# A routed expert layer on one core: the down matrix laid out eight rows per partition and brought in one transfer, the activations transposed in 64 by 64 blocks

## The reference

```python
def expert_block(args):
    xb, e = args
    gu = xb @ w_gu[e] + b_gu[e]                 # 1024 x 2048 per expert, 8 MB
    g = jnp.minimum(gu[:, :D_EXPERT], SWIGLU_LIMIT)
    lin = jnp.clip(gu[:, D_EXPERT:], -SWIGLU_LIMIT, SWIGLU_LIMIT)
    glu = g * jax.nn.sigmoid(SWIGLU_ALPHA * g)
    return ((lin + 1.0) * glu) @ w_down[e] + b_down[e]   # 1024 x 1024 per expert, 4 MB
```

## Time and profile before

| | |
|---|---|
| median of 3 runs | 1186.44 us (1186.06 to 1187.45) |
| profiled execution | 1186.64 us |
| its span | 1184.9 us |
| granted TensorE clock, mean of the span | 0.982 |
| PE busy | 1101.6 us (93%) |
| PEld busy | 582.4 us (49%) |
| DVE busy | 392.4 us (33%) |
| ACT busy | 247.0 us (21%) |
| moved by DMA | 452.07 MB, mean 382 GB/s |

### The profile page before, as it was taken

The page is one execution under the profiler, slowest core; times in us unless marked ns, Lnnn a source line. Parts: engine busy times, 40 slices in busy tenths (PEclk is TensorE's granted clock), DMA queues, the critical chain, the costliest instruction groups (busy, mean ns, idle before and its releaser), DMA issues.

```text
span 1184.9 us, 14766 instructions
## 1 busy us (share of the span) xinstructions
PE 1101.6 (93%) x6066; PEld 582.4 (49%) x6066; DVE 392.4 (33%) x649; ACT 247.0 (21%) x389; POOL 4.5 (0%) x10
## 2 busy tenths in 40 slices
PE   8999999999999898989889898899899988998995
PEld 8999999984433333333333333333343333333331
DVE  6768655563222222222222222222222222222223
ACT  6444773432111111111111111111111111111112
POOL 0000000000000000000000000000000000000000
PEclk9999999999999999999999999999999999999998
DMA  9984444689999999999999999999999999999996
GB/s 328 349 280 159 160 161 159 252 320 402 416 414 431 430 430 431 430 431 431 431 436 428 428 436 429 428 435 429 428 435 429 427 436 423 430 431 430 414 424 257
DMA packets 60407, 452.07 MB, mean 382 GB/s; under 512 B 3490, under 2 KB 34455, under 8 KB 40535
## 3 DMA queue, kind: packets, MB, share of 16 engines
q1 hardware_dynamic: 59696, 449.79, 91.9%
q0 software_dynamic: 560, 1.74, 0.5%
q10 hardware_dynamic: 119, 0.08, 0.0%
HBM read 450.53 MB, written 1.06 MB: 381 GB/s over the span
## 4 chain that ended last, share of the span: by engine, by line
DMA 50%; PE 45%; SPq 1%; ACT 1%; DVE 1%; issue 1%; DVEq 0%
DMA dring<-in_w_down_dram 43%; PE bank L1146 17%; PE bank L1497 13%; PE bank L1444 10%; DMA ring<-in_w_gu_dram 6%; PE bank L1411 1%; DMA ring<-in_w_mem_kv_dram 1%; PE bank L1356 1%; PE bank L1237 0%; PE bank L1458 0%; PE bank L1386 0%; SPq L310 0%; ACT w_high L472 0%; PE bank L1549 0%; PE bank L1258 0%
## 5 line engine op out<-in xcount | busy, mean ns | idle before, releaser
L1444 PE MATMUL bank<-ring,region_x 128*64 128x512 f32 x2048 | 456.0, 597 | 6.6 <-DMA ring<-in_w_gu_dram 6.6
L1497 PE MATMUL bank<-dring,region_r 128*64 128x512 f32 x1024 | 245.1, 628 | 61.2 <-DMA dring<-in_w_down_dram 60.6
L1444 PEld LDWEIGHTS bank<-ring,region_x 128*64 128x64 f32 x2048 | 141.4, 137 | 280.7 <-issue 265.8
L1497 PEld LDWEIGHTS bank<-dring,region_r 128*64 128x64 f32 x1024 | 73.2, 143 | 230.2 <-issue 130.8
L1146 PE MATMUL bank<-hT_high,w_high 128*128 128x256 f32 x384 | 109.9, 286 | 1.3 <-DVE hT_low L727 1.3
L1146 PE MATMUL bank<-hT_high,w_low 128*128 128x256 f32 x384 | 108.7, 283 | 0.0
L1146 PE MATMUL bank<-hT_low,w_high 128*128 128x256 f32 x384 | 108.7, 283 | 0.0
L735 DVE TENSOR_TENSOR w_low<-ring,w_high 128x2048 fp32r<-128x2048 f32 x39 | 89.3, 2289 | 52.5 <-ACT w_high L472 52.4
L1052 DVE TENSOR_SCALAR region_r<-bank 128x512 f32<-128x512 f32 x32 | 22.1, 691 | 253.7 <-PE bank L1444 253.7
L1071 DVE SCALAR_TENSOR_TENSOR y_parts<-bank,region_r,y_parts 64x512 fp32r<-64x512 f32 x32 | 23.8, 744 | 224.0 <-ACT y_parts L644 224.0
L472 ACT ACTIVATE w_high<-ring 128x2048 fp32r<-128x2048 f32 x39 | 74.5, 1912 | 55.7 <-PE bank L1146 51.2
(11 more groups left out here) (241 smaller groups left out, 863.1 us busy)
## 6 DMA issues: line engine op xcount, KB each, us to landing
ring<-in_w_gu_dram SPq DMA_DIRECT2D x52, 4096.0 KB, 26.3
dring<-in_w_down_dram SPq DMA_DIRECT2D x56, 2048.0 KB, 25.1
ring<-in_w_gu_dram SPq DMA_DIRECT2D x17, 2048.0 KB, 11.5
ring<-in_w_in_dram SPq DMA_DIRECT2D x26, 1024.0 KB, 11.8
dring<-in_w_down_dram SPq DMA_DIRECT2D x16, 1024.0 KB, 11.9
ring<-in_w_gu_dram SPq DMA_DIRECT2D x14, 1024.0 KB, 7.9
ring<-in_w_out_dram SPq DMA_DIRECT2D x4, 1024.0 KB, 4.7
ring<-in_w_mem_kv_dram SPq DMA_DIRECT2D x3, 1024.0 KB, 12.3
```

What stands on the lines that cost most here:

```text
L1444: last = mm(ps[64 * half:64 * half + 64, :], xg[u // 2][:, c, 64 * (u % 2):64 * (u % 2) + 64], ring[:, slot0 + c, k * F + half * 512:k * F ...
L1497: last = mm(ps[64 * half:64 * half + 64, :], lhsT, dring[:, c // 2, at:at + 512], start=(c == 0), stop=(c == KC - 1))
```

## The change

A partition of `dring` held, for each half of the down matrix, four of its rows (4p to 4p+3 of that half). Now partition p holds rows 8p to 8p+7 of the whole matrix. The matrix is one run of 32 KB per partition, and `expert_down` brings it in one transfer of 4 MB instead of two of 2 MB, when all four pieces of the matrix before are used. The 1 MB pieces at the start and the end remain, with the new rows.

The left operand of `down` must follow: partitions 0 to 63 of a chunk need the activations of the first 512 columns, 64 to 127 those of the last 512. These are the halves in which `g_sb` has them. So `hidden_transposed` transposes 64 by 64 blocks, the lower half to the lower partitions, the upper to the upper: 16 ordinary products with a part of the identity in place of 4 transposes. L1059 writes with a stride of 8 instead of 4 at its source. In `small_products`, and at the last expert, the slots are now transposed ahead of the activations.

```diff
-            m, k = j // 2, j % 2
             sp.dma_start(dring[:, j:j + n, :].rearrange("p k n -> p (k n)"),
-                         a["w_down"][0, bass.ds(expert, 1), m * 512:(m + 1) * 512, :]
-                         .rearrange("e (p k) n -> p (e k n)", k=4)[:, k * PIECE:(k + n) * PIECE]).then_inc(down_in[j], 16)
-
-        def expert_down(expert, uses, n=2):
+                         a["w_down"][0, bass.ds(expert, 1), :, :]
+                         .rearrange("e (p k) n -> p (e k n)", k=KC)[:, j * PIECE:(j + n) * PIECE]).then_inc(down_in[j], 16)
+
+        def expert_down(expert, uses, n=DRING):
...
-            dve.tensor_tensor(hid_by_row, hid_fours, sg_fours, ALU.mult).then_inc(hid_ready, 1)
+            dve.tensor_tensor(hid_by_row, hid_eights, sg_eights, ALU.mult).then_inc(hid_ready, 1)
...
-            for c in range(4):
-                last = transpose(tr_ps[:, c * P:(c + 1) * P], g_sb[:, c * P:(c + 1) * P], ident)
+        def hidden_transposed():
+
+            for c in range(KC):
+                for m in range(2):
+                    half = slice(64 * m, 64 * m + 64)
+                    last = mm(tr_ps[half, 64 * c:64 * c + 64], g_sb[half, 64 * c:64 * c + 64], ident[half, half],
+                              start=True, stop=True)
             last.then_inc(hidT_done, 1)
...
             s = i * 4 + u
-            hidden_transposed(s, halves)
+            pe.wait_ge(hid_ready, s + 1)
+            pe.wait_ge(xg_sb, s + halves)
             pe.wait_ge(y_ready, s + 1)
             slots_transposed(s, y_ps)
+            hidden_transposed()
             scatter_of(s - 1, (u + 1) % 2)
...
             for c in range(KC):
-                if c % 4 == 0:
-                    pe.wait_ge(down_in[c // 2], (s + 1) * 16)
+                if c == 0:
+                    pe.wait_ge(down_in[0], (s + 1) * 16)
                 elif c % 2 == 0:
                     pe.wait_ge(down_in[c // 2], 16 + 16 * single)
-                lhsT = hidT[:, (c % 4) * P + 64 * (c // 4):(c % 4) * P + 64 * (c // 4) + 64]
+                lhsT = hidT[:, 64 * c:64 * c + 64]
...
         s = i * 4 + 3
-        hidden_transposed(s, 1)
+        pe.wait_ge(hid_ready, s + 1)
+        pe.wait_ge(xg_sb, s + 1)
         slots_transposed(s, lin_ps)
+        hidden_transposed()
         down(s, 3, gate_ps, lambda: scatter_of(s - 1, 0))
```

More of the change, by code:

```diff
@@ L224, in build @@
     hidT = region_r[:, 3072:3584]
[L225 to L228, removed]
+    in_eights = "p (q k) -> p k q"
+    hid_eights = hid.rearrange(in_eights, k=KC)
+    sg_eights = sg.rearrange(in_eights, k=KC)
+    hid_by_row = g_sb.rearrange("p (k q) -> p k q", k=KC)
     x2T = region_r[:, 0:2048].rearrange("p (c t) -> p c t", c=KC)
@@ L1451, in up @@
                     later()
-        def hidden_transposed(s, halves):
-            pe.wait_ge(hid_ready, s + 1)
-            pe.wait_ge(xg_sb, s + halves)
-            for c in range(4):
-                last = transpose(tr_ps[:, c * P:(c + 1) * P], g_sb[:, c * P:(c + 1) * P], ident)
+        def hidden_transposed():
[4 more added lines that the diff above has]
+                              start=True, stop=True)
             last.then_inc(hidT_done, 1)
```

## The result

| | before | changed |
|---|---|---|
| median of 5 runs | 1186.44 us (1185.88 to 1187.45) | 1193.11 us (1192.15 to 1194.34) |
| ratio, 95% interval | | 1.0053 (1.0042 to 1.0064) |
| profiled execution, its span | 1186.64, 1184.9 us | 1193.32, 1191.5 us |

The changed kernel is slower by 6.7 us. I had forecast 1187.0 in a range of 1184.0 to 1190.2, so this is a miss.

A forecast was written before the change was run, and what follows sets the result against it. Transfers were taken to bound the kernel from some 355 us on, TensorE having slack. Terms -2.0 + 1.4 + 0.9 + 0.3 = +0.6 us gave 1187.0 us against 1186.44, range 1184.0 to 1190.2.

The forecast's parts named there:

- What bounds the kernel: Some 800 us paced by transfers: 29.22 us of transfers per expert against 25.09 of TensorE, whose slack is 4.1 us.
- -2.0 for the single transfer: Down loads of 28 experts: one 4 MB transfer instead of two of 2 MB saves 0.07 us each, -2.0 us.
- DVE with stride 8, 0: VectorE's gate product, 1094 ns, read only some 16 us later: even doubled it stays hidden, 0 us.
- x: Extra TensorE time per expert for the 64 by 64 transposes: +0.7 us, hidden in the steady stretch.
- A: Rival, slower: small products cost their issue or do not overlap, 1.5 to 1.8 us extra per expert; about 1190 us, chance 0.14.
- B: Rival: TensorE becomes the bound, with 3.8 us extra per expert for the transposes; +10.6 us, 1197 us, chance 0.03.
- (a): Queue hole at 328 us, where a gate/up issue waits behind two sets of transposes: +1.4 us, never won back.
- (b): At the end, the last down product waits for slots' transposes moved ahead (0.22 us) and slower block transposes: +0.9 us.
- At least 10.8 us to spare. No hole: Steady stretch: the later 4 MB down issue still finds 8 MB of gate/up queued, 19.4 us, so no transfer time is lost.
- The third last product, +0.3: Near the end, this down product starts 2.5 us late, 2.3 us are won back, 0 to 0.8 remain: +0.3 us.
- Rival D: At the end, whole-matrix waits start the third last product late, clock falls, nothing won back: +2.9 us, 1189.3 us, chance 0.09.
- the other two signs: Forecast wrong if landing distance moves over 0.15 us or the transposes' extra per expert exceeds 1.3 us.

The follow-up runs named there:

- mixed: Changed kernel with 4 MB down transfers and whole waits for experts 2 to 19, two 2 MB transfers with split waits for 20 to 29: 1189.66 us.
- halves: Changed kernel, its transposes and layout kept, with the down matrix again in two 2 MB transfers issued and waited for by halves: 1188.50 us.
- before_blocks: Kernel before with only the 64 by 64 transposes in their new place, its old layout, two transfers and split waits kept: 1188.44 us.
- after_mid: Changed kernel with two 2 MB down transfers and split waits for experts 20 to 25 only: 1191.11 us.
- use_halves: Changed kernel with two 2 MB down transfers; SP waits for the whole matrix to be used before issuing both, TensorE waits by halves: 1188.53 us.
- issue_halves2: Changed kernel with two 2 MB down transfers, SP issuing by halves, TensorE waiting for both, except for the last two experts, taken piece by piece: 1190.87 us.
- before_late: Kernel before with its small products (transposes, scatter) behind the fourth gate/up chunk instead of the third: 1187.18 us.

## Why the prediction was wrong, point by point

*What bounds the kernel*: right for the kernel before and for the steady stretch. In the changed kernel TensorE takes over again at 1134.6 us and sets the pace to the end.

*-2.0 for the single transfer*: right in rate, 0.07 us per expert (466.31 us over 16 experts against 467.49). Whether any of it reaches the end no run shows: mixed had it and was slower than halves.

*DVE with stride 8, 0*: right. The operation takes 1092 ns in the changed kernel, 1096 before (medians of 32), and the layout costs nothing in halves against before_blocks.

*x = +0.7*: 0.81 to 0.84. The 32 instructions took 1.08 us, 34 ns each against my 27; the rest (0.3) is longer slots' transposes and scatter beside the changes of shape. Rivals A (x from 1.3) and B fall. The Trainium skill (TensorE: Matmul & The Clock Gate, Back-to-back issue gap) gives about 62 ns per matmul with hardware decode off, by which 32 would have taken about 1.98 us; the 1.08 does not agree with that figure.

*(a) The hole at 328 us, +1.4*: right. +1.3 by the landings, and the issue 1.65 us later relative to the mixer's end.

*(b) The last transposes, +0.9*: right; 1168.78 to 1171.00 is 2.22 us against 1.35 between 1163.43 and 1164.78. The slots' transposes took 0.37 there in place of my 0.22. The two together with x are what before_blocks measured as 2.0 us, where I would have said 2.3.

*"At least 10.8 us to spare. No hole"*: **this step failed.** I read the cover behind a landed down matrix from the loop, at 652 us, where it is 8 MB, and applied it to all experts. But where the order changes, the cover is 4 MB, 9.72 us, at two places: behind expert 19, where the down matrix of 20 moves between the two halves of gate/up, and behind expert 24, where that of 25 follows one half alone. Against it stand a product at the low clock (8.76 us, a size I had in the same paragraph), and the 3.6 to 3.8 us by which an issue must come ahead of the landing of its cover, which I had left out: 9.7 - 8.8 - 3.8 is -2.9, where I had 10.8 to spare. Expert 24, with its product at 7.09, has 9.7 - 7.1 - 3.8 = -1.2. It cost 3.8 us by landings and windows. Taking only these holes away gave 2.0 us back (after_mid, with the doubt named there), and the holes need both whole waits: either alone has none (use_halves, issue_halves2).

*The third last product, +0.3*: mis-sized. I had it start 2.5 us late, lose up to 1.7 to the clock, and win back 2.3. The win came, but the product was slower than I allowed: 10.03 us from the landing, 3.2 above full speed, so it ended 3.8 us later against the landing than before, where I had 0.7 to 2.4. With 0.8 for x and about 2.5 won back (1.7 of it seen, 0.8 eaten by x) 2.1 remain. The ledger has +3.1 behind 1135 us, of which 0.9 are (b), so 2.2 against 0.3. Rival D's size for this place was near it (2.6), but not its reason: the pieces of the last matrix did come late (1163.67 us and on), and cost TensorE at most 0.3 us. D's total of +2.9 lacked the holes, and the sum of both is what was measured: -1.2 (by the ledger up to expert 19) + 1.3 + 0.9 + 2.2 + 3.7, with the start 0.6 earlier, = +6.3, against 6.7 in the profiled executions (1193.32 and 1186.64).

*What would show me wrong*: I named gate/up waits in the steady stretch. They did not come, since the lost time sat in the queue while TensorE had work. Nor did the other two signs: the distance of landings moved by 0.08 us, and x stayed under 1.3. The slices of GB/s were the view that showed it.

**Open**: why after_mid gave back 2.0 us and not the length of the holes (the runs spread over 3.3 us); how much the clock, low in the product of expert 19 in one run and not in another, adds to the holes and to that spread; what in before_late makes transfers slower before 300 us. No version tried beat the kernel before.

## What to carry to other kernels

When a transfer and its buffer's release are merged, two waits become whole at once, and the queue must hold other transfers for the time of the product and some 4 us more (here 3.6 to 3.8, an estimate from two places). Work that margin out at the place where the order of transfers gives the least cover, which need not be the loop. A busy TensorE hides a dry queue: in a kernel bound by transfers read the GB/s of each stretch, and count what is lost there even when nobody waits. The clock can be low in the product behind a wait (before and after the change), and the cover has to be taken with the slow product.

## What the runs showed of the hardware

- 32 instructions of 64 by 64 by 64 in fp32 (16 products, alternating between two diagonal tiles) took 1.08 us, 34 ns each. Full 128-column ones take 122 ns.
- A 4 MB transfer with 32 KB per partition moves 4 MB in 9.72 us, or 2.43 us per MB, whether it is gate/up or down; 16 KB takes 2.445, 8 KB 2.49. Row length and size of the transfer change together here (4, 2 and 1 MB), so no run parts them. The place in DRAM did not count: 2 MB halves land 29.21 us per expert apart in halves (420.75 to 449.96), 29.22 before.
- Of 20 down products of the changed kernel that waited for their 4 MB, each started 0.47 to 0.50 us behind the end of the transfer's last packet. The 16 engines did not end together: the last was 0.7 to 2.2 us behind the first. The Trainium skill (DMA: Bandwidth & Descriptors, Anatomy of one DMA) puts about 2 us of fixed cost on a transfer, most of it behind the last byte, for transfers issued in software; these, issued by SP, show 0.5 us behind the last packet.
- With an empty queue the first data came 1.0 us behind the issue (867.05 and 866.08), and the first packets of 32 KB took 1.4 to 2.3 us, against 1.2 in a full queue. An issue 0.9 us ahead of the landing of the last queued transfer cost 2.7 us of the queue's time, one 2.6 us ahead 1.2 us.
- Between 362 and 858 us, 8 of 18 down products of the changed kernel ran at the 1.2 GHz level for part of their time (8.4 to 10.0 us against 7.09), all behind a wait of 3.0 us for the matrix (two others with such a wait kept the full level); in after_mid it was also 8 of 18. The kernel before has the same, 8 products of 8.7 to 8.8 us behind waits of 2.3 to 2.5 us. In halves, whose waits are 1.65 us at most, there is none, and the granted clock over 360 to 858 us is 1.00 there against 0.97 in the other two. The runs of halves lie 0.6 us apart, those of after_mid 3.3 and of the changed kernel 2.2; that the clock makes this spread is not shown.
